# Seven places for the first modulation blocks and an early inverse root, together with rearranged joints in a gated scan

## The reference, cut to what matters

```
m = silu(cond) @ w_ada[layer] + b_ada[layer]      # (1024) @ (1024 x 6144): shift, scale, gate, twice
h = modulate(rmsnorm(x, norm_mix[layer]), sh_m, sc_m)   # x * rsqrt(mean(x*x)+eps) * gain * (1+scale) + shift
y = even_mixer(h, ...)                            # layer 0: projection, DFT mixing, gMLP, output projection
p = h @ w_in                                      # layer 1: q, g, and z_f, z_b, i for two directions
o, _, _ = bidir_scan(q, i, fw, bw, s_f, s_b)      # HGRN2: gated linear recurrence both ways, 8 heads
x = x + g_m * rec_output(o, g, rec_norm, w_out_odd)     # RMS norm per head, times silu(g), projection
```

## Time and profile before

| what | value |
|---|---|
| median of 3 runs | 1897.21 us (1896.88 to 1897.9) |
| device time of the profiled execution | 1895.47 us |
| span of its trace | 1893.6 us, so 1.87 us lie around it |
| mean granted clock of TensorE | 0.969 of full |
| PE busy | 1764.3 us, 93% of the span |
| DVE busy | 853.6 us, 45% |
| ACT busy | 690.6 us, 36% |
| read from HBM | 477.03 MB, mean 252 GB/s |

### The profile page before, as it was taken

The page is one execution under the profiler, slowest core; times in us unless marked ns, Lnnn a source line. Parts: engine busy times, 40 slices in busy tenths (PEclk is TensorE's granted clock), DMA queues, the critical chain, the costliest instruction groups (busy, mean ns, idle before and its releaser), DMA issues.

```text
span 1893.6 us, 28155 instructions
## 1 busy us (share of the span) xinstructions
PE 1764.3 (93%) x11488; PEld 1312.9 (69%) x11488; DVE 853.6 (45%) x1197; ACT 690.6 (36%) x893; POOL 3.5 (0%) x6
## 2 busy tenths in 40 slices
PE   5899899999999988998979999999989999998987
PEld 2568677888887878977867887775536887763433
DVE  2524433534533466567538985554203565420011
ACT  3323532222224545445357864454003454400001
POOL 0000000000000000000000000000000000000000
PEclk8899999999999999999979999999999999999998
DMA  8654166533731232121138979999999999999995
GB/s 319 248 197 147 43 216 229 188 100 123 244 96 61 89 91 87 47 81 42 67 134 284 376 287 398 408 409 409 408 409 405 400 408 407 408 408 409 409 409 237
DMA packets 161843, 479.96 MB, mean 253 GB/s; under 512 B 14976, under 2 KB 58160, under 8 KB 155568
## 3 DMA queue, kind: packets, MB, share of 16 engines
q1 hardware_dynamic: 161712, 478.14, 66.7%
HBM read 477.03 MB, written 1.05 MB: 252 GB/s over the span
## 4 chain that ended last, share of the span: by engine, by line
PE 68%; DMA 15%; DVE 7%; ACT 4%; SPq 3%; issue 2%; DVEq 0%; ACTq 0%
PE ps L641 16%; PE ps L643 15%; PE ps L642 15%; DMA arena<-in_moe_up 5%; PE ps L1374 4%; DMA arena<-in_moe_w 4%; DMA raw<-in_moe_up 3%; PE ps L1445 3%; SPq L590 3%; DMA raw<-in_moe_w 3%; DVE w_lo L1924 3%; PE ps L655 2%; PE ps L1363 1%; PE ps L1195 1%; PE ps L679 1%
## 5 line engine op out<-in xcount | busy, mean ns | idle before, releaser
L1924 DVE TENSOR_TENSOR w_lo<-raw,w_hi 128x1024 fp32r<-128x1024 f32 x242 | 293.9, 1223 | 353.2 <-ACT w_hi L1538 349.4
L1538 ACT ACTIVATE w_hi<-raw 128x1024 fp32r<-128x1024 f32 x242 | 253.3, 1056 | 445.5 <-PE ps L643 351.7
L641 PE MATMUL ps<-h_hi,w_hi 128*128 128x512 f32 (+1 forms) x736 | 284.8, 387 | 15.6 <-DVE h_lo L2018 10.8
L642 PE MATMUL ps<-h_hi,w_lo 128*128 128x512 f32 (+1 forms) x736 | 277.4, 377 | 0.0
L643 PE MATMUL ps<-h_lo,w_hi 128*128 128x512 f32 (+1 forms) x736 | 277.3, 377 | 0.0
L1924 DVE TENSOR_TENSOR w_lo<-arena,w_hi 128x1024 fp32r<-128x1024 f32 x144 | 173.9, 1223 | 101.5 <-ACT w_hi L1538 96.7
L1538 ACT ACTIVATE w_hi<-arena 128x1024 fp32r<-128x1024 f32 x144 | 152.3, 1060 | 128.4 <-DMA arena<-in_moe_up 65.0
L641 PEld LDWEIGHTS ps<-h_hi,w_hi 128*128 128x128 f32 x736 | 142.4, 193 | 59.6 <-issue 35.2
L643 PEld LDWEIGHTS ps<-h_lo,w_hi 128*128 128x128 f32 x736 | 141.8, 193 | 25.6
L642 PEld LDWEIGHTS ps<-h_hi,w_lo 128*128 128x128 f32 x736 | 142.6, 194 | 23.7 <-issue 0.5
L641 PE MATMUL ps<-w_hi,s_hi 128*128 128x512 f32 x336 | 134.9, 401 | 4.6 <-DVE s_lo L2447 2.4
(11 more groups left out here) (357 smaller groups left out, 2269.1 us busy)
## 6 DMA issues: line engine op xcount, KB each, us to landing
arena<-in_moe_up SPq DMA_DIRECT2D x256, 512.0 KB, 11.3
raw<-in_moe_up SPq DMA_DIRECT2D x192, 512.0 KB, 11.1
arena<-in_moe_w SPq DMA_DIRECT2D x128, 512.0 KB, 13.8
raw<-in_moe_w SPq DMA_DIRECT2D x96, 512.0 KB, 14.6
arena<-in_w_ada SPq DMA_DIRECT2D x36, 1024.0 KB, 5.1
raw<-in_ffn_w SPq DMA_DIRECT2D x66, 512.0 KB, 5.8
raw<-in_w_in_odd SPq DMA_DIRECT2D x40, 512.0 KB, 3.5
scratch<-in_w_ada SPq DMA_DIRECT2D x12, 1024.0 KB, 5.9
```

The source lines that it names most:

```text
L641: pe.matmul(dst, s_h, m_h, start=start, stop=False, **kw)
L642: pe.matmul(dst, s_l, m_h, start=False, stop=False, **kw)
L1538: act.activation(w_hi[:, o % R, :], src, ACT.Copy).then_inc(hi_done, 1)
L1924: dve.tensor_tensor(w_lo[:, o % R, :], src, w_hi[:, o % R, :].bitcast(F32), ALU.subtract).then_inc(lo_done, 1)
```

## The change

It has two parts, made together.

*Beginning.* The first seven modulation blocks have a place each: two in `raw`, one in `scratch`, four in the arena; block 7 takes the place of block 0. Each of the eight has a semaphore of its own (`first_in`). Blocks 8, 9 and 10 wait for the use of blocks 2, 5 and 6 instead of the end of the norm. Even unit 0 is issued after six blocks, unit 1 after eight, units 2 to 5 after the use of blocks 3 and 4. ACT writes the squares to eight places, and the inverse root is made by Ln and Exp on ACT. DVE multiplies five tiles of x by it ahead of `coef`, and the other three between the first tiles. The sums of squares stand between the first three blocks on PE.

*Scan.* `cross(g)` of the first two groups stands behind the last projection unit instead of ahead of it. In the last group `outputs(2)` and what follows on it come one step later, behind `diagonal` and level 0. The six splits of output units that stood among the end of the third group on ACT and DVE move into steps 2 to 4 of the last group. The gates of the first group come about one step earlier.

```
+            if a < KT:
+                return first_in[a], 16
...
+        def first_slot(a):
+            if a in (3, 4):
+                return raw[:, 2 * a - 4:2 * a - 2, :].rearrange("p a c -> p (a c)")
+            return scratch[:, :] if a == 2 else ar((4096, 10240, None, None, None, 6144, 8192, 4096)[a], A_COLS)
...
         def units_before(g, k):
             if g < NG - 1:
-                return U_IN_ODD + G_UNITS * (g + 1) + k
+                return min(U_IN_ODD + G_UNITS * (g + 1) + k, U_OUT_ODD - 1 - LEAD)
+            if g == NG - 1 and k < OUT_SLOT:
+                return U_OUT_ODD - 1 - LEAD + (0, 0, 2, 4)[k]
             return U_OUT_ODD + (min(max(k - OUT_SLOT, 0), 6) if g == NG - 1 else 6)
...
-                if a == 10:
-                    sp.wait_ge(ada_used, 8)
+                if a < KT + A_SLOTS:
+                    if a >= KT - 1:
+                        sp.wait_ge(ada_used, (1, 3, 6, 7)[a - KT + 1])
...
-                if a in (9, 10):
-                    sp.wait_ge(h_done, KT)
...
-            ada_unit(0, 1, True, False)
-            ada_unit(1, 1, False, False)
-            norm_sum(0, NT)
-            for a in range(2, KT):
-                ada_unit(a, 1, False, a == KT - 1)
+            for a in range(KT):
+                ada_unit(a, 1, a == 0, a == KT - 1)
+                for i in ((0, 1), (2, 3), (4, 5, 6, 7), (), (), (), (), ())[a]:
+                    first_sum(i)
...
+                    late = int(g == NG - 1)
-                    if k == 1 and end:
+                    if k == 1 and end and not late:
                         outputs(g - 1)
...
+                    if k == 2 and late:
+                        outputs(g - 1)
...
-                    if k == 9 and rec:
+                    if k == 9 and rec and g >= NG - 2:
                         cross(g)
...
+                    if k == 9 and rec and g < NG - 2:
+                        cross(g)
...
+            for kt in range(5):
+                first_inv(kt)
+            split_to(1)
             ada_cols(0, 2)
             dve.wait_ge(ada_done, 1)
-            norm_dve(0, NT, 0, V_NMIX, SH_M, SC_M, 2)
+            norm_coef(0, V_NMIX, SC_M)
+            first_norm()
...
-                    if k == 7 and proj:
+                    if k == (7 if p else 6) and proj:
                         for d in range(2):
                             gate_logs(p, d)
...
-                    if k == 9 and proj:
+                    if k == (9 if p else 8) and proj:
                         for d in range(2):
                             gate_floor(p, d)
                             context(p, d)
```

More of the change, by code:

```diff
@@ L389, in ada_landed, with square_at @@
             place = ada_place(a)
-            return ada_in[place], 16 * sum(ada_place(b) == place for b in range(a + 1))
+            if a < KT:
+                return first_in[a], 16
+            return ada_in[place], 16 * sum(ada_place(b) == place for b in range(KT, a + 1))
+        def first_slot(a):
+            if a in (3, 4):
+                return raw[:, 2 * a - 4:2 * a - 2, :].rearrange("p a c -> p (a c)")
+            return scratch[:, :] if a == 2 else ar((4096, 10240, None, None, None, 6144, 8192, 4096)[a], A_COLS)
+        def square_at(i):
+            return ar(X_ROWS + i * NT, NT)
         def ada_slot(a):
+            if a < KT:
+                return first_slot(a)
             at = A_SLOT_AT[a // KT]
@@ L405, in moe_seen @@
             k = n % M_RING
-            earlier = len(range(k, U_MOE, R)) if k < R else 0
+            earlier = len(range(k, U_MOE, R)) if k < R else 1
             return moe_in[k], 16 * (earlier + n // M_RING + 1)
@@ L1128, in _ @@
                         level(g, k - 2)
-                    if k == 3 and end:
+                    if k == 2 and late:
+                        outputs(g - 1)
+                    if k == 3 + late and end:
                         pe.wait_ge(o_sq, g)
@@ L1747, in _ @@
                         act.activation(ar(base(g) + R_G, G_LAT), ps[:, 3, :], ACT.Silu).then_inc(g_rdy, 1)
-                    if k == 2 and end:
+                    if k == 2 + late and end:
                         act.wait_ge(o_mm, g)
@@ L1754, in _ @@
                         turned_copy(g, 0)
-                    if k == 3 and proj:
+                    if k == (3 if p else 2) and proj:
                         gate_out(p, 0)
@@ L1765, in _ @@
                         act.activation(std, std, ACT.Exp, scale=-0.5).then_inc(o_std, 1)
-                    if k == 5 and proj:
+                    if k == (5 if p else 4) and proj:
                         gate_out(p, 1)
-                    if k == 5 and end:
+                    if k == 5 + late and end:
                         for h in range(HG):
@@ L1778, in _ @@
                         act.activation(ar(base(p) + R_V, TT * HG * P), ps[:, 0:2, :], ACT.Copy).then_inc(v_rdy, 1)
+                    if k == (6 if p else 5) and proj:
                         gate_soft(p)
@@ L1781, in _ @@
                             act.activation(lnlb[:, :], lb1[:, :], ACT.Ln).then_inc(lnlb_in, 1)
-                    if k == 8 and proj:
+                    if k == (8 if p else 7) and proj:
                         act.wait_ge(lnlb_rdy, 1)
@@ L2276, in _ @@
                         widen(g, k - 2)
-                    if k == 4 and end:
+                    if k == 4 + late and end:
                         o32 = o_part(g - 1, 0)
@@ L2293, in _ @@
                                               ALU.subtract).then_inc(rlo_done, 1)
-                    if k == 5 and proj:
-                        for d in range(2):
+                    for d in range(2):
+                        if k == (5 if p else 3 + d) and proj:
                             gate_abs(p, d)
-                    if k == 7 and proj:
+                    if k == (7 if p else 6) and proj:
                         for d in range(2):
```

96 lines of the change are left out of this document (45 added, 51 removed).

## The result

| | median, us | runs | ratio to before, 95% interval |
|---|---|---|---|
| before | 1897.05 | 4, 1896.87 to 1897.9 | |
| changed | 1869.28 | 4, 1866.47 to 1876.01 | 0.9863 [0.9849, 0.9877] |
| changed, a second time | 1873.09 | 4, 1869.73 to 1875.77 | 0.9875 [0.9860, 0.9891] (before: 1895.96) |

The change makes the kernel 1.3% faster. The profiled execution took 1867.23 us, 28.2 us less than that of before; 30.1 was the forecast. The runs lie further apart than before; the experiments show in which stretch the time differs.

The account below looks back on a forecast made before the run. TensorE bounds the kernel up to the experts, then the expert weight stream does. Beginning 14.7, gates 8.3, `cross` 0, last joint 10.5, less clock 3.4, make 30.1 us: 1865.4 for the profiled execution, median 1867.1, range 1860 to 1877.

Parts of the forecast that it names:

- Block 7: Beginning: with seven places, bytes in at 33.1, block usable at 34.3, products 1.93 us at half clock; 6.3 us earlier.
- T: Beginning: the time when block 7's products are done and the row is whole; 42.48 before, 36.2 forecast.
- First tiles: From `coef` to the first low part: one DVE product of two goes, 0.7 us gained.
- the stop: PE's wait at block 9, issued only after the norm, with slow clock after it: goes, gaining 7.7 us.
- Gates: First gates in the scan: turned keys no longer wait, 6.6 us plus 1.7 of slow clock; 8.3 us gained.
- `cross` in groups 0 and 1: Behind the last unit: its wait goes, `outputs` wait about 2.6 and 4.2 us for DVE's chain; order costed at nothing.
- The last joint: Third group's end into last group: moved splits and later outputs gain 10.5 us, bounds 3.6 and 11.2.
- The clock in the scan: Four waits left or new: two bring half clock at 1.7 us each, costing 3.4 us, between 0 and 6.8.
- The stream moves with PE: Experts: their weight stream starts after scan and norm, so PE's gain ahead moves it forward as a whole.

Follow-up runs that it names:

- The kernels of the table: Before, the changed kernel (run twice) and eleven further kernels with parts of the change, edits put back, dummy products or split gathering; medians from 1859.21 to 1903.76 us.
- the gathering in pieces: Changed kernel with dummies in the scan, plus the first expert turn's second gathering issued in three pieces between units: 1868.63 us, ratio 0.9857, against 1871.06 without the pieces.

## Why the prediction was right

The time (1869.28 for 1867.1, in the range) is right, and the waits go and come where I said; the terms are not all right, and some errors cancel. That the sum is so close is in part luck, as the terms below show.

- *Block 7.* I had it usable at 34.3 and T = 36.2. It ran at 35.91 and T was 36.97, a lead of 5.5 instead of 6.3 us. The four windows add up to 12.5 MB, where my step counted 11.36: 1.2 MB more had moved, so units issued behind block 7 took part of the rate. The full clock gave back 0.9 us of it. The 1.1 us from last byte to use can't be checked here, since the bytes were off by more.
- *First tiles and the stop.* 0.7 us was said for the tiles; the lead grew by 7.66 - 5.51 = 2.2, and 15.05 us stood at block 10 for 14.7. From the first product to block 10 the lead grew by 15.05 - 7.66 = 7.4 us, near the 7.7 of the term; putting the stop back into the changed kernel, whose norm ends earlier, costs 5.4 to 6.7.
- *A gain I didn't have.* 1.16 us come between the DFT and the odd projection, all of it behind the second layer norm, where the half clock was shorter: a mean clock of 0.87 for 0.76 over the 12 us behind its wait of 5.39 us, and 0.76 again in the second profile of the changed kernel. The kernels of the table take 476.7 to 478.2 us from one to the other, and 475.5 with dummies ahead of the norms' first products, and the changed kernel itself 478.0 in its second profile. So this is the clock's doing and no part of the change.
- *Gates.* 8.98 us for 8.3. With the scan's half alone it is 9.06 - 0.63 = 8.4, the lead at level 6 of group 0 less that at the odd projection.
- *`cross` in groups 0 and 1.* The waits at `outputs` were 2.89 and 2.99 for 2.6 and 4.2 (1.54 and 2.93 in the second profile), `cross` had none, and the run with `cross` put back shows that DVE's chain sets them. Costed at nothing for the order, rightly.
- *The last joint.* 10.5 us were said, 27.72 - 21.79 = 5.9 measured. Level 1 has a lead of 9.6 us over the count from level 5 (11.2 said), level 2 of 9.9, and then 3.9 us go lost up to level 4, where a level, a sum and an output unit ran 8.95 us at a clock of 0.62. The two spells of this group cost 1.7 + 3.4 = 5.1 us; without them it would be 11.0. The mechanism holds, and the two edits need each other, as the chain of the step had it.
- *The clock in the scan* is the term that was mis-sized. I took two of four waits, 3.4 us, and bounded it by 6.8, each at the 1.7 us of the earlier trace rows. Behind all four the clock fell, and behind one of them it cost double: 1.7 + 1.7 + 1.7 + 3.4 = 8.5 us. This is 5.1 more than said, and beyond my bound. The other terms were 3.2 better than said, which is why the sum is off by only 1.9 us. That is luck in part: 1.2 of the 3.2 are the clock's between DFT and projection, and this profile has the shortest tail of all, 897.1 us. The Trainium skill (TensorE: Matmul & The Clock Gate, Why this matters for your kernels) says that waits between bursts bring the half rate back. The trace agrees at these four, with 2.16 to 3.08 us of waiting at each. It doesn't do so everywhere: in the second profile the first of them was 1.54 us long and left full clock, and the 2.97 us ahead of `cross` of group 1, in the trace that I had, left it too, which my step overlooked. So the count of four was a matter of chance as well.
- *The stream moves with PE.* Right on the average, 27.75 at the first expert product and 28.2 at the end. But this step took the tail as fixed, and it isn't: 897.1 to 906.2 us over these profiles.

## What to carry to other kernels

A wait taken away is worth its length plus the slow clock behind it, and a wait put in its place costs the same way: price each wait that is left, of the length seen here (2.16 to 3.08 us), as 1.7 to 3.4 us of lost clock if PE is the bound behind it, and take that as likely rather than certain. When a lead shows in the trace at one product and not in the time, compare the same products down the whole program, kernel by kernel; the difference lies between the last product where it is there and the first where it isn't. Two edits of one chain can each lose alone and gain together, so test them apart before dropping one.

## What the hardware showed

Two executions of the same program reached the same product at 968.33 and 968.40 us and ended 8.6 us apart. 8.4 of them are 3.4 MB that the slower one's stream was behind, at or just after half-clock spells of a PE that the stream waits for. The same length of waiting was followed by half clock in some places and executions and not in others: 2.97 us ahead of `cross` of group 1 left a clock of 1.00 over the next 8 us in the kernel before and with the beginning only, 2.96 us at the same place one of 0.81 with `cross` put back. And dummy products at eight waits, useless as work, made the kernel faster by 0.5% (1859.71 for 1869.28 us, ratios 0.9808 and 0.9863). What makes the clock fall on a PE that doesn't wait stays open. It fell within the gathering in some executions and not in others, of one and the same kernel, and in none with the gathering in pieces; three profiles are too few to call that the cause.
